# Two SBUF buffers lose 16 columns of padding each, and what lies behind them moves by 64 to 192 bytes

## The reference

```python
for i in range(4):                     # first block
    h = (mixer_a, mixer_b, mixer_c)[i % 3](x, ...)      # window, dilated, block attention
    x = layer_norm(DN_ALPHA * x + h, ...)
    x = layer_norm(DN_ALPHA * x + swiglu(x, w_gate_up[i], w_down[i]), ...)
for l in range(2):                     # second block
    h = rmsnorm(x, attn_norm_g[l])
    proj = h @ w_in[l]                 # 1024 -> gating, SSM, attention and gate columns
    y_a, y_b, y_c = spatial_gating(...), mamba2_mixer(...), diff_attention(...)
    merged = g0 * (y_a @ w_branch_a[l]) + g1 * (y_b @ w_branch_b[l]) + g2 * (y_c @ w_branch_c[l])
    x = x + merged @ w_out[l]
    up = causal_dwconv(rmsnorm(x, ...) @ ffn_w_up[l], ...)
    x = x + (silu(gate) * val) @ ffn_w_down[l]

def swiglu(x, w_gate_up, w_down):      # D_FF = 2816
    gu = x @ w_gate_up
    return (silu(gu[..., :D_FF]) * gu[..., D_FF:]) @ w_down
```

## The kernel before

| class | triples | streamed, start | loaded, start |
|---|---|---|---|
| A, `tok`, first block's mixers | 480 | `whi`/`wlo` 0 | `xh` 0, `xl` 128 |
| B, `tok`/`row`, all others from `xh`/`xl` | 352 | `whi`/`wlo` 0 | `xh` 224, `xl` 96 |
| C, `row`, from `oh`/`ol` | 656 | `whi`/`wlo` 0 | `oh`, `ol` 128 |
| D, `col`, from `xh`/`xl` | 2560 | `xh` 224, `xl` 96 | `whi`/`wlo` 0 |
| E, `col`, from `oh`/`ol` | 256 | `oh`, `ol` 128 | `whi`/`wlo` 0 |

## Time and profile before

### The profile page before, as it was taken

How to read it: one execution, slowest core, us unless ns; L and a number is a source line. 1 busy time by engine, 2 the same in 40 slices (tenths; PEclk the granted TensorE clock), 3 DMA queues, 4 the chain that set the end, 5 groups by cost and what they waited for, 6 DMA issues and landing times.

```text
span 2449.2 us, 36757 instructions
## 1 busy us (share of the span) xinstructions
PE 2351.1 (96%) x15344; PEld 2089.2 (85%) x15344; DVE 1512.1 (62%) x2421; ACT 1257.9 (51%) x1792; POOL 327.1 (13%) x307
## 2 busy tenths in 40 slices
PE   7999999999999999999999979989999999899999
PEld 6799878787899777998789968889899898898998
DVE  6754555555744647447665477465776675566775
ACT  5544365554444455444544456464555575554654
POOL 0100022211100313001010003323000023430000
PEclk9999999998999999999999989999999999999999
DMA  6255543332455534555255544324455453345553
GB/s 256 101 201 186 183 155 139 137 123 101 172 189 189 187 123 155 186 187 200 89 187 189 189 141 153 138 104 172 173 188 190 169 178 135 122 155 172 189 186 125
DMA packets 58182, 398.94 MB, mean 163 GB/s; under 512 B 6816, under 2 KB 7072, under 8 KB 11680
## 3 DMA queue, kind: packets, MB, share of 16 engines
q1 hardware_dynamic: 56864, 393.75, 45.0%
q10 hardware_dynamic: 1152, 2.83, 0.3%
HBM read 395.51 MB, written 1.05 MB: 162 GB/s over the span
## 4 chain that ended last, share of the span: by engine, by line
PE 61%; DVE 7%; ACT 3%; issue 2%; POOL 2%; DVEq 0%; ACTq 0%; POOLq 0%
PE b L1166 12%; PE b L1168 11%; PE b L1167 11%; PE b L1099 7%; PE b L1101 7%; PE b L1100 7%; PE b L1104 4%; PE b L1108 2%; ACT whi L1463 2%; DVE wlo L1805 1%; DVE b L1830 1%; POOL xn L2501 1%; DVE st L1892 1%; DVE b L1889 0%; DVE xn L1904 0%
## 5 line engine op out<-in xcount | busy, mean ns | idle before, releaser
L1805 DVE TENSOR_TENSOR wlo<-raw,whi 128x2048 fp32r<-128x2048 f32 x362 | 838.7, 2323 | 504.0 <-ACT whi L1463 503.6
L1463 ACT ACTIVATE whi<-raw 128x2048 fp32r<-128x2048 f32 x362 | 689.4, 1912 | 459.4 <-PE b L1168 242.3
L1166 PE MATMUL b<-xh,whi 128*128 128x256 f32 x2560 | 725.9, 284 | 1.0 <-ACT PT L1463 1.0
L1168 PE MATMUL b<-xh,wlo 128*128 128x256 f32 x2560 | 714.6, 279 | 0.0
L1167 PE MATMUL b<-xl,whi 128*128 128x256 f32 x2560 | 714.3, 279 | 0.0
L1166 PEld LDWEIGHTS b<-xh,whi 128*128 128x128 f32 x2560 | 482.9, 189 | 7.1 <-issue 4.7
L1167 PEld LDWEIGHTS b<-xl,whi 128*128 128x128 f32 x2560 | 483.5, 189 | 2.1
L1168 PEld LDWEIGHTS b<-xh,wlo 128*128 128x128 f32 x2560 | 483.5, 189 | 0.0
L1099 PE MATMUL b<-whi,xh 128*128 128x512 f32 x832 | 342.3, 411 | 31.8 <-DVE xl L1838 16.1
L1101 PE MATMUL b<-whi,xl 128*128 128x512 f32 x832 | 330.5, 397 | 0.0
L1100 PE MATMUL b<-wlo,xh 128*128 128x512 f32 x832 | 329.8, 396 | 0.0
(11 more groups left out here) (228 smaller groups left out, 2624.9 us busy)
## 6 DMA issues: line engine op xcount, KB each, us to landing
raw<-in_w SPq DMA_DIRECT2D x362, 1024.0 KB, 4.8
gt<-in_rows SPq DMA_DIRECT2D x8, 512.0 KB, 4.0
bt<-in_rows SPq DMA_DIRECT2D x8, 512.0 KB, 5.1
abq<-in_rows ACTq DMA_DIRECT2D x2, 768.0 KB, 6.4
x<-in_x SPq DMA_DIRECT2D x1, 1024.0 KB, 6.3
bc<-in_rows SPq DMA_DIRECT2D x4, 256.0 KB, 4.9
out<-x SPq DMA_DIRECT2D x4, 256.0 KB, 2.1
msk<-in_masks SPq DMA_DIRECT2D x1, 768.0 KB, 6.4
```

Source lines behind the costliest of these rows:

```text
L1166: pe.matmul(out, wh[:, k, cs], ah[:, kk, :], start=kk == 0 and s == 0, stop=False, skip_group_check=True)
L1168: last = pe.matmul(out, wl[:, k, cs], ah[:, kk, :], start=False, stop=final and k == 3, skip_group_check=True)
L1463: return ac.activation(out, i, ACT.Copy)
L1805: ve.tensor_tensor(B.wlo[r][:, :], B.raw[r][:, :], B.whi[s][:, :], ALU.subtract).then_inc(sem["loV"], 1)
```

## The change

`xh` and `xl` lose 16 of their 32 spare columns each, and `S` 16 of its 24 spare ones. None of these columns is read or written.

```diff
-        self.acts = sb("xh", [128, 2080], F32R), sb("xl", [128, 2080], F32R)
+        self.acts = sb("xh", [128, 2064], F32R), sb("xl", [128, 2064], F32R)
...
-        big = sb("S", [128, 1568])
+        big = sb("S", [128, 1552])
```

## The result

| | before | changed |
|---|---|---|
| median | 2452.45 us (4 runs) | 2468.45 us (4 runs, 2465.97 to 2469.73) |
| ratio | | 1.006, 95% interval 1.0048 to 1.0073 |
| profiled execution, span | 2449.2 us | 2464.3 us |

The kernel became slower by 0.6%: by 16.0 us between these two medians, by 14.9 us if the changed kernel's other executions on record are taken in (21 in all, median 2467.31 us, which fits the ratio of 1.006), and by 15.1 us between the two profiled spans. The direction was as forecast, the size was not: 2457.5 us and a range of 2445 to 2467 had been given, and both medians lie above it.

The account below looks back on a forecast made before the run. The prediction took TensorE's pace of gapless matmuls as the bound. Its terms, +6.9 + 1.4 - 1.1 + 0 - 0.7 = +6.5 us on 2451.04, gave 2457.5 us, with an 8-in-10 range of 2445 to 2467.

Parts of the forecast that it names:

- What bounds the kernel: Long FFN stretches: TensorE's pace of gapless matmuls sets the end; the other engines' work stays covered, value 0.
- Which addresses count: All triples of matmuls: pace depends on operand addresses, by up to 6 ns in 700 and 5.4 in 351.
- The first rival: All classes: only starts modulo 64 count, so every pace stays and nothing changes; 2451.0 us, chance 0.33.
- A: 512-column triples, mostly from `xh` in the first block: 694 ns, +3 ns x 480 = +1.4 us.
- B: Slowest 512-column triples, in `tok` and `row`: 700 ns, -3 ns x 352, -1.1 us.
- Term D: 256-column triples in the FFNs' `col`: from 351.3 ns, +2.7 ns x 2560 = +6.9 us; bounds -5.1 to +13.8.
- E: Slower 256-column triples, same loaded operand, other streamed starts: 356.7 ns, -2.7 ns x 256, -0.7 us.
- C: 512-column triples loading `oh` and `ol`: middle pace 697 ns, 656 triples, value 0, bounds +-2.0 us.
- The loads: Loads of `raw`, now starting off a 256-byte boundary: cost 0, hidden by the ring's slack; skill-based estimate 0.08 us each.
- The second rival: B, C and E gain together -5.5 us while D and A hold: 2445.5 us, chance 0.20.
- The third rival: D falls to E's pace and A to B's, +16.7 us less 1.8: 2466 us, chance 0.11.

Follow-up runs that it names:

- all_96: Kernel before plus an unused 96-byte buffer ahead of `xh`, shifting `xh` and everything behind it with all distances kept; 2452.59 us, ratio 0.9998.
- minus_64: Kernel before, re-laid with unused columns so `xh`, `xl`, `oh` and `ol` start 64 bytes below the weights modulo 256; 2423.47 us, 0.9882 of before.
- acts_only: Half of the change on the kernel before: `xh` and `xl` 16 columns narrower, `S` left as it was; 2458.55 us, ratio 1.0027.
- break_64: Changed kernel, addresses kept, with one extra 64-column matmul at the start of a group of `col` (92 in all); 2463.21 us, ratio 1.0049 to before.
- minus_64_break: minus_64 with the extra 64-column matmuls at the start of groups of `col`; 2453.20 us in its one run.
- acts_oh_192: acts_only with `oh` and `ol` moved forward by 64 bytes, where the change moves them back; 2451.75 us, ratio 0.9998 to before.

## Why the prediction was right, and where it was wrong

**What bounds the kernel**: right. Only TensorE's paces moved the time of the changed kernel; splitting, ScalarE's writes to `xh` and `oh` (597 and 598 ns) and loads kept theirs within 1 ns and 0.1 us.

**Which addresses count**: right that distances modulo 256 do. The first rival (only starts modulo 64 count) fell with the changed kernel itself, and all_96 shows that the starts as such are nothing. That nothing but the distances counts, which the expectations call theory 1, was wrong. The prediction reads from the earlier trace rows that a matmul streams while the next one's weights are loaded, and then pairs each matmul with its own weights; in all five classes both ways give the same three distances, in A and B only in another order, so nothing hangs on it.

**Term D: the step that failed.** It was given +2.7 ns, with E's pace as the upper bound (+5.4, 13.8 us). Measured is a mean of +6.0 ns x 2560 = +15.4 us, made of two paces, +2.2 and +8.9. There were two errors in that one step. The bound was the slowest pace that the trace happened to show in a class with other addresses, which excludes nothing about a new set. And the step took the pace as a function of the addresses alone, though the rows spoke against it: the earlier trace rows are one class with one set of addresses at 351.3 and 353.3 ns. I read their 2.0 ns as scatter, and used it as a lower bound. It was the sign of a second thing that sets the pace, what the engine ran before, and that is worth 6.7 ns in the changed kernel and 13.3 in minus_64. With D at 353.3 throughout, as in acts_only, the term would have been +5.6, near the +6.9 forecast; that nearness is luck, since D does not move towards E's pace but takes two of its own.

**Terms A, B, C, E.** A: +6.7 ns x 480 = +3.2 us (forecast +1.4, upper bound 2.9). B: -6.7 x 352 = -2.3 (forecast -1.1, bound -2.1). C: +2.9 x 656 = +1.9 (forecast 0, inside its bounds). E: -2.7 x 256 = -0.7, as forecast. Without D these come to +2.1, where -0.4 was forecast. With D the paces give +17.5, and the triples' steps really lengthened by 15.7, since some of A and B stands beside waits. A and B exchanged their paces, though not their distances: each has a set that neither had before.

**The loads**: right, at nothing. The Trainium skill (DMA: Bandwidth & Descriptors, "How a descriptor splits into AXI transactions") would add some 0.08 us a load, an estimate; the median is 4.8 us in both, which doesn't resolve that, and no engine waited longer for `raw`.

**The second rival** (small classes gain and D holds) had the mechanism half right: B and E gained 3.0 us together. C lost 1.9, and D did not hold.

**The third rival** (D at the slow end, 2466 us, chance 0.11) came nearest in time, and not by its mechanism. It put D at one pace, E's 356.7 ns, because its new set has no 32 left. D stood at 353.3 and 360, and acts_only has the same set and only 353.3.

## What to carry to other kernels

Where a kernel streams matmuls without a gap, read its pace from starts, by class of operands, and look whether one class shows two paces: if it does, neither addresses nor instruction alone explain it, and a change elsewhere (here, in the place of buffers that D does not read, `oh` and `ol` among them) can move the costliest class by several ns a triple. Padding of a few bytes is then worth an experiment rather than a calculation: it was worth +0.6% in this change and -1.2% in minus_64, with no instruction changed. Halves of such a change do not add, and an interval taken from paces already seen is too narrow for a new layout.

## What was not expected of the hardware

- Three matmuls of 256 columns took 340, 351.1, 353.3, 355.6 or 360 ns, three of 512 took 686.7 to 700, at the full clock, by the operands' distances modulo 256 bytes and by what ran before. The Trainium skill (TensorE: Matmul & The Clock Gate, "Step-by-step: what each phase is for") has the streamed operand and the next weights read by two independent ports; 340 against 353.3 ns at the same instruction does not agree with that as the whole story. What inside the engine makes the two interact these runs do not show, nor which part of what ran before picks the pace.
- The steady pace holds on: once entered, at 360 or 353.3 ns, it lasted for all 96 matmuls of a group, and one matmul of 64 columns ahead of the group was enough to change it, to the better in break_64 and to the worse in minus_64_break.
- The clock can hide or feign a few microseconds of a change: between traces of these kernels, steps at the lower level took 6.4 us more (minus_64), 5.7 more (acts_oh_192), 3.0 more (all_96, with unchanged paces) or 0.4 less (changed) than before. A difference of that size is to be read from the steps, not from the time.
